# A residual add at three branch ends, with 512 of its columns moved from VectorE to GpSimd

## The reference

```python
mod = silu(c) @ w_ada + b_ada                 # 9 vectors of 2048
h = modulate(rmsnorm(x, g_ffn1_pre), sh1, sc1)
y = rmsnorm(swiglu(h, w1_gate, w1_up, w1_down), g_ffn1_post)
x = x + 0.5 * gt1 * y
h = modulate(rmsnorm(x, g_mix_pre), sh2, sc2)
y = hybrid_mixer(h, ...)                      # two kinds of attention, one output projection
x = x + gt2 * rmsnorm(y, g_mix_post)
h = modulate(rmsnorm(x, g_ffn2_pre), sh3, sc3)
y = rmsnorm(swiglu(h, w2_gate, w2_up, w2_down), g_ffn2_post)
x = x + 0.5 * gt3 * y
```

## Time and profile before

| | us |
|---|---|
| median of three runs | 1909.19 |
| the runs | 1906.36 to 1914.8 |
| the profiled execution, its own time | 1911.35 |
| its span, first to last instruction | 1909.5 |
| TensorE busy | 1856.0 (97%) |
| VectorE busy | 1339.0 (70%) |
| ScalarE busy | 894.4 (47%) |
| GpSimd busy | 0.2 |
| bytes read from memory | 485.04 MB, 255 GB/s over the span |

### The profile page before, as it was taken

The page is one execution under the profiler, slowest core; times in us unless marked ns, Lnnn a source line. Parts: engine busy times, 40 slices in busy tenths (PEclk is TensorE's granted clock), DMA queues, the critical chain, the costliest instruction groups (busy, mean ns, idle before and its releaser), DMA issues.

```text
span 1909.5 us, 24544 instructions
## 1 busy us (share of the span) xinstructions
PE 1856.0 (97%) x8980; PEld 1558.7 (82%) x8980; DVE 1339.0 (70%) x1593; ACT 894.4 (47%) x1135; POOL 0.2 (0%) x4
## 2 busy tenths in 40 slices
PE   6999999999999999899999998999999999999998
PEld 6888888888887787689988786888888888888886
DVE  5888877788888877679785787777544454444444
ACT  4677644344444333644446546444444444434443
POOL 0000000000000000000000000000000000000000
PEclk9999999999999999899999998999999999999999
DMA  9998888899989988588992594988766666566653
GB/s 375 404 350 279 260 270 275 286 331 328 330 301 328 349 306 307 172 245 286 299 310 97 166 319 133 308 286 278 229 188 188 192 191 187 176 193 193 194 192 132
DMA packets 264875, 488.45 MB, mean 256 GB/s; under 512 B 21718, under 2 KB 32332, under 8 KB 264524
## 3 DMA queue, kind: packets, MB, share of 16 engines
q1 hardware_dynamic: 263904, 486.67, 76.5%
q10 hardware_dynamic: 876, 0.53, 0.1%
HBM read 485.04 MB, written 2.10 MB: 255 GB/s over the span
## 4 chain that ended last, share of the span: by engine, by line
PE 89%; DVE 3%; DMA 3%; DVEq 2%; ACT 2%; issue 1%; ACTq 0%; SPq 0%
PE pair L1430 27%; PE pair L1432 26%; PE pair L1431 26%; PE tps L1488 2%; DMA raw<-in_w_down 2%; PE pair L1454 2%; PE pair L1457 2%; PE pair L1456 2%; DVE start_acc L950 1%; DMA start_raw<-in_w_ada 1%; DVEq L949 1%; PE mps L1526 1%; DVE w_lo L918 1%; ACT w_hi L571 1%; PE mps L1556 1%; DVE acc L937 1%
## 5 line engine op out<-in xcount | busy, mean ns | idle before, releaser
L571 ACT ACTIVATE w_hi<-raw 128x1024 fp32r<-128x1024 f32 x634 | 668.7, 1057 | 908.7 <-PE pair L1432 482.2
L918 DVE TENSOR_TENSOR w_lo<-raw,w_hi 128x1024 fp32r<-128x1024 f32 x634 | 770.1, 1218 | 420.4 <-ACT w_hi L571 416.1
L1430 PE MATMUL pair<-w_hi,h_hi 128*128 128x512 f32 (+1 forms) x1664 | 651.6, 392 | 5.5 <-DVE w_lo L918 4.3
L1432 PE MATMUL pair<-w_hi,h_lo 128*128 128x512 f32 (+1 forms) x1664 | 646.7, 389 | 0.0
L1431 PE MATMUL pair<-w_lo,h_hi 128*128 128x512 f32 (+1 forms) x1664 | 646.1, 388 | 0.0
L1430 PEld LDWEIGHTS pair<-w_hi,h_hi 128*128 128x128 f32 x1664 | 313.3, 188 | 69.5 <-issue 3.4
L1432 PEld LDWEIGHTS pair<-w_hi,h_lo 128*128 128x128 f32 x1664 | 313.2, 188 | 64.6
L1431 PEld LDWEIGHTS pair<-w_lo,h_hi 128*128 128x128 f32 x1664 | 313.4, 188 | 61.9
L937 DVE SCALAR_TENSOR_TENSOR acc<-raw,c_col,acc 128x512 f32<-128x512 f32 x420 | 315.7, 752 | 48.2 <-DMA raw<-in_w_ada 13.2
L1430 PE MATMUL pair<-w_hi,hid_hi 128*128 128x512 f32 x704 | 277.1, 394 | 1.3 <-DVE w_lo L918 1.0
L1432 PE MATMUL pair<-w_hi,hid_lo 128*128 128x512 f32 x704 | 274.2, 390 | 0.0
(11 more groups left out here) (192 smaller groups left out, 845.5 us busy)
## 6 DMA issues: line engine op xcount, KB each, us to landing
raw<-in_w_ada SPq DMA_DIRECT2D x224, 512.0 KB, 5.1
raw<-in_w_gate SPq DMA_DIRECT2D x176, 512.0 KB, 4.4
raw<-in_w_up SPq DMA_DIRECT2D x176, 512.0 KB, 4.1
raw<-in_w_down SPq DMA_DIRECT2D x176, 512.0 KB, 4.5
start_raw<-in_w_ada SPq DMA_DIRECT2D x64, 512.0 KB, 7.5
raw<-in_w_in SPq DMA_DIRECT2D x56, 512.0 KB, 4.5
raw<-in_w_o SPq DMA_DIRECT2D x32, 512.0 KB, 5.2
raw<-in_w_uq SPq DMA_DIRECT2D x12, 256.0 KB, 4.6
```

Source lines behind the costliest of these rows:

```text
L571: nc.scalar.activation(w_hi[:, w % HI_RING, :, 0:n], raw[:, r % RING, :, 0:n], ACT.Copy).then_inc(hi_ready, 1)
L918: nc.vector.tensor_tensor(w_lo[:, r % RING, :, 0:n], raw[:, r % RING, :, 0:n], w_hi[:, w % HI_RING, :, 0:n], ALU.subtract).then_inc(raw_us ...
L1430: nc.tensor.matmul(o, hi, wh, start=first and kk == 0, stop=False, skip_group_check=added)
L1432: ins = nc.tensor.matmul(o, lo, wh, start=False, stop=last and kk == 1, skip_group_check=added)
```

## The change

At each branch end VectorE's first half of tile 1 begins at column 512 instead of column 0, so this instruction is 128 x 512 and VectorE adds 1536 of the 2048 columns of that tile. GpSimd does columns 0 to 511: it waits for the refined root of tile 1, multiplies those columns of `y` by it in place, drains, and adds them to `x`, counting up a new semaphore `x_pool`. ScalarE's `square_x` waits for `x_pool` besides `x_ready` before piece 2, and SyncE does so before the third output store. Tile 0 is as it was.

```diff
+        x_pool = sem("x_pool")
...
                 sp.wait_ge(x_ready, 4 * 2 + n + 1)
+                if n == TT:
+                    sp.wait_ge(x_pool, 3)
                 sp.dma_start(out[t * P:(t + 1) * P, c], x[:, t, c]).then_inc(out_stored, 16)
...
                     act.wait_ge(x_ready, 4 * {N_X1: 0, N_XM: 1}[k] + n + 1)
+                    if n == TT:
+                        act.wait_ge(x_pool, {N_X1: 1, N_XM: 2}[k])
...
                     for h in range(2):
-                        c = slice(h * XB, (h + 1) * XB)
+                        c = slice(NB if t and not h else h * XB, (h + 1) * XB)
                         nc.vector.scalar_tensor_tensor(x[:, t, c], y[:, t, c], rstd[:, of_t], x[:, t, c],
                                                        ALU.mult, ALU.add).then_inc(x_ready, 1)
...
+        @block.gpsimd
+        def _(pool):
+            for k in (N_Y1, N_YM, N_Y2):
+                pool.wait_ge(ref_ready, k + 2)
+                nc.gpsimd.tensor_scalar(y[:, 1, 0:NB], y[:, 1, 0:NB], rstd[:, 1:2], None, ALU.mult)
+                pool.drain()
+                nc.gpsimd.tensor_tensor(x[:, 1, 0:NB], x[:, 1, 0:NB], y[:, 1, 0:NB], ALU.add).then_inc(x_pool, 1)
```

## The result

The changed kernel takes 1920.08 us (median of 7 runs, 1918.31 to 1926.53) beside 1910.96 us for the kernel before (7 runs): ratio 1.0049, 95% interval 1.0032 to 1.0066. A second timing, later, gave 1.0048 (1.0032 to 1.0064). The change costs some 9 us; the forecast was 4.2 us. The profiled execution has a span of 1924.7 us.

What follows compares the result with a forecast made beforehand. TensorE was taken as the bound, waiting at branch ends on VectorE's add, ScalarE's squares and the normalising. Three ends losing 1.4 us each, 4.2 us, on the 1909.2 us median gave 1913.4 us; range 1908.4 to 1920.5 us.

Steps and rivals of the forecast that it cites:

- What bounds the branch end: TensorE waits at the branch end; ScalarE idles only 0.20 us before square 2, so an earlier half add gains at most that.
- The removed 512 columns buy nothing: VectorE's first tile 1 add shrinks from 1.28 to 0.64 us; at the first two ends this buys at most 0.2 us.
- GpSimd's price: At each branch end GpSimd's multiply and add of 512 columns were priced at 1.28 us each, 2.56 us together.
- no interference: GpSimd works beside VectorE unhindered; each branch end loses about 1.4 us, whole kernel 1911.3 to 1915.5 us; chance 0.46.
- Rival B: After the root, GpSimd and VectorE's two-operand instructions get in each other's way and GpSimd comes last; chance 0.38 over all forms.
- middle form: GpSimd's multiply enters after VectorE's half add, its add after VectorE's second; 3.3 us per end; range 1914 to 1919, chance 0.25.
- B's full form: GpSimd reads only after VectorE's adds and subtraction; 4.5 us lost at two ends, 3.3 at the third, 1921.5 us; chance 0.13.
- Third end: At the last branch end the third store goes about 1.4 us later, shifting the whole store burst and the kernel's end.
- The low case: GpSimd at VectorE's prices, 1.17 us: square 2 keeps its place at the branch ends, about -0.8 us in all, 1908.4 us.

Runs made afterwards that it cites:

- the run with 256 columns: GpSimd given 256 instead of 512 columns against the changed kernel, VectorE adding 768 and then 1024 columns beside it; one execution took 1918.05 us.
- the best placement: Against the changed kernel, GpSimd takes the last 512 columns of tile 0 instead of the first of tile 1; ratio 1.0007 to the kernel before.

## Why the prediction was right or wrong

**What bounds the branch end: right.** ScalarE had sat idle for 0.2 us before tile 1's first square, so this square followed its half of the add at once, and each microsecond by which GpSimd came later reached TensorE's gap: 3.33 us at the square, 3.31 and 3.32 in the gaps.

**The removed 512 columns buy nothing: right.** VectorE's short add was over at 804.19 and ScalarE free at 804.62 in the profile after; it waited for GpSimd alone. The add of 512 columns was taken for 0.64 us and has 0.75, which changes nothing.

**GpSimd's price: the term that was mis-sized.** I took 1.28 + 1.28 us. Alone the two take 1.56 + 1.26, so the add was right and the multiply 0.28 us short; that is a small part of the 1.9 us by which GpSimd was late against the forecast. The estimate from the Trainium skill (GPSIMD Engine Reference, Elementwise) of 0.77 us for the multiply is half of what these runs show, its 1.12 us for the add 10% short.

**The step that failed: "no interference".** In the forecast GpSimd worked beside VectorE as if alone, done 2.66 us after its start. It was done after 4.55 us. By the runs: 1.56 + 0.14 + 1.26 = 2.96 us for itself, 0.54 us behind VectorE's half add (2.10 - 1.56), and 1.05 us behind the weight subtraction (2.31 - 1.26). At the third end the last part is missing and it is 3.51 us. So the waits for VectorE are 1.6 of the missing 1.9 us, and the loss per end was 3.3, 3.3 and 2.3 us, not 1.4 each.

**Rival B, in its middle form, is what happened**, with a chance of 0.25 in the text: GpSimd gets in between VectorE's instructions, "each end loses 3.3 us". The way to that figure was another, and that it fits is partly luck. I had GpSimd's add wait for VectorE's second add, and that one held up by the whole multiply. In truth the second add was held only 0.35 us, ran beside most of the multiply, and GpSimd's add met the subtraction; the dearer multiply made up the rest. At the third end, which has no subtraction, this form of B also had 3.3 us, and 2.3 were measured. B's full form, in which GpSimd comes last, is excluded: in the kernel after, the multiply was over at 805.54, before VectorE's second add (805.74), and in the run with 256 columns GpSimd's add went ahead of the subtraction. The rule of the Trainium skill (SBUF — State Buffer, two separate sides), that the first to come locks the shared ports for a whole instruction, holds for GpSimd behind a VectorE instruction with two operands and for VectorE's subtraction behind GpSimd's add (0.52 of 0.59 us). It doesn't hold for VectorE behind GpSimd's multiply: 1.35 us of it were left, and VectorE was held 0.35.

**Third end: the way was right, the size not.** The third store's wait shifted the whole burst by 2.3 us, where GpSimd's lateness against the old end of VectorE's first half (3.51 - 1.28) is 2.2.

**Slips in the sums.** "2.66 us after the root" is 2.66 us after GpSimd's start and 2.76 after the root by the text's own terms; the sum uses it rightly. The low case doesn't come out: 0.6 + 0.2 + 0.2 is 1.0 us and not 0.8, and at VectorE's prices GpSimd would be done 1.27 us after its start, when the third store's half was ready anyway (1.28 us), so the third end would have given nothing. The lower bound of 1908.4 us has nothing under it; the measured time doesn't touch it.

**Time and chances.** 1920.1 us lies at the upper end of the range (1908.4 to 1920.5). It is there by B's middle form and not by the forecast, whose own range ended at 1915.5: the mechanism taken as likeliest, with 0.46, was wrong, and its loss too small by a factor of two. Of the 6.7 us between 1913.4 and 1920.1 the missed loss is 4.9; 1.8 come from the kernel before, whose median rose from 1909.19 to 1910.96 us with four more runs. In the second timing the same change had a median of 1922.8 us beside 1912.4, outside the range with the same ratio; that the absolute time fell inside is luck. The text took 0.5% as the least that can be told from no change, but the interval, +0.32 to +0.66%, leaves out no change. The text had the row for doubt: VectorE without a gap in its instructions just where GpSimd works. It should have weighed B above a forecast for which no row spoke either.

No version here beats the kernel before: the best placement equals it.

One rival isn't tested. Every wide VectorE instruction that GpSimd met had two operands, so the runs show that GpSimd waits for these, and not that it would pass a wide one with a single operand. The small step with one operand that was held speaks for caution.

## What to carry to other kernels

Before work goes from VectorE to GpSimd, look at what VectorE does in the same microseconds: here GpSimd waited for all of each two-operand instruction that had begun before it or with it, so its time is its own plus what it meets. Then ask for the deadline of that piece: the same 512 columns cost 3.3 us per end where the next engine wanted them 1.4 us after VectorE's adds began, 2.1 us where it wanted them after 2.6, and nothing where it wanted them after 4.5 (tile 0's second square in the kernel before). Where the path doesn't wait for VectorE, as here, relieving it brings nothing in the best case.

## What the runs showed of the hardware

- GpSimd on 128 partitions of float32, from 256 and 512 columns: a multiply by a per-partition scalar takes 0.92 and 1.56 us (0.28 us + 2.5 ns per column), an add of two tiles 0.72 and 1.26 us (0.18 us + 2.1 ns per column). VectorE needs 0.48 us for such a multiply and 0.69 us for a subtraction of two tiles at 512 columns.
- A GpSimd multiply that starts with a two-operand VectorE add ends 1.35 us after it (512 columns; 2.10 beside 0.75, 2.63 beside 1.28), and lengthens VectorE's next add by 0.35 us; with 256 columns it ends 0.71 us after it (1.73 beside 1.02) and lengthens the next add by 0.14 us (1.42 instead of 1.28).
- Between GpSimd's add and VectorE's subtraction the earlier goes first, in both directions: GpSimd's add 1.26 to 2.31 us behind a subtraction, a subtraction 1.22 to 1.74 us behind GpSimd's add of 256 columns.
- A one-operand VectorE step on two elements per partition took 0.78 instead of 0.17 us under GpSimd's add; one on a single element was not held.
